# Decoder trunk with hierarchical experts: running sum of x held in four PSUM banks, 21 weight slots, down weights loaded behind the next set's up weights

## The reference, cut to what matters

```
x = x + concat(diff_attention(h), stick_breaking(h)) @ w_out      # h = rms_norm(x) @ w_in
h2 = rms_norm(x)
combine[token, expert] = router weights: best of 4 groups, then best 2 of its 8 experts
x = x + sum over 32 experts e of
        (silu(h2 @ w_gate[e]) * (h2 @ w_up[e]) * combine[:, e]) @ w_down[e]
```

## Time and profile before

| | us |
|---|---|
| median of 3 runs (752.16 to 755.38) | 753.58 |
| the profiled execution | 752.93 |
| its span, first to last instruction | 751.1 |
| PE busy | 662.4 (88%) |
| DVE busy | 302.4 (40%) |
| ACT busy | 126.0 (17%) |
| share of the DMA engines taken by the weight queue | 79.7% |

### The profile page before, as it was taken

How to read it: one execution, slowest core, us unless ns; L and a number is a source line. 1 busy time by engine, 2 the same in 40 slices (tenths; PEclk the granted TensorE clock), 3 DMA queues, 4 the chain that set the end, 5 groups by cost and what they waited for, 6 DMA issues and landing times.

```text
span 751.1 us, 12265 instructions
## 1 busy us (share of the span) xinstructions
PE 662.4 (88%) x4720; PEld 359.2 (48%) x4721; DVE 302.4 (40%) x617; ACT 126.0 (17%) x298; POOL 8.5 (1%) x18
## 2 busy tenths in 40 slices
PE   7999999998898896595899999999887989975856
PEld 4444556475554452432344454656744535523522
DVE  0345654154453542331325267421633435432413
ACT  3114442220000000000031154314100010000000
POOL 0000200000000000000020000000000000000000
PEclk8999999999999998987999999999999999988979
DMA  8796635546999999999999531394289999999995
GB/s 314 247 368 267 160 113 224 219 173 244 419 421 422 421 422 421 422 422 420 361 361 399 229 115 54 136 368 176 82 361 421 423 391 419 422 422 422 421 405 221
DMA packets 52918, 239.05 MB, mean 318 GB/s; under 512 B 7760, under 2 KB 8048, under 8 KB 29328
## 3 DMA queue, kind: packets, MB, share of 16 engines
q1 hardware_dynamic: 52416, 238.09, 79.7%
q0 software_dynamic: 464, 0.47, 0.9%
HBM read 237.49 MB, written 1.05 MB: 318 GB/s over the span
## 4 chain that ended last, share of the span: by engine, by line
PE 67%; DMA 19%; DVE 5%; issue 4%; SPq 2%; DVEq 2%; ACT 1%; ACTq 0%
PE bank L1153 21%; DMA wbuf<-in_w_down 18%; PE bank L1338 11%; PE bank L1306 8%; PE bank L1250 7%; PE bank L1350 5%; PE bank L1281 5%; PE bank L1317 2%; DMA wbuf<-in_w_in 1%; PE bank L1230 1%; PE bank L1173 1%; SPq L355 1%; PE bank L1210 1%; PE bank L1257 1%; PE bank L1184 1%
## 5 line engine op out<-in xcount | busy, mean ns | idle before, releaser
L1153 PE MATMUL bank<-wbuf,hTbuf 128*128 128x512 f32 x384 | 171.2, 602 | 4.1 <-DMA wbuf<-in_w_in 3.7
L1338 PE MATMUL bank<-wbuf,qkT 128*32 128x512 f32 x512 | 73.3, 721 | 54.0 <-DMA wbuf<-in_w_down 47.2
L1153 PEld LDWEIGHTS bank<-wbuf,hTbuf 128*128 128x128 f32 x384 | 72.6, 193 | 91.8 <-issue 87.8
L1306 PE MATMUL bank<-wbuf,qkT 128*32 128x256 f32 x2048 | 113.8, 380 | 2.3 <-DVE qkT L843 2.3
L1306 PEld LDWEIGHTS bank<-wbuf,qkT 128*32 128x32 f32 x2048 | 65.2, 110 | 54.3 <-issue 10.6
L1281 PE MATMUL bank<-qkT,xn 128*128 128x128 f32 x512 | 63.0, 282 | 10.6 <-issue 9.8
L879 DVE TENSOR_TENSOR x_sb<-x_sb,bank 128x512 f32<-128x512 f32 x72 | 49.5, 687 | 50.9 <-PE bank L1350 50.9
L1281 PEld LDWEIGHTS bank<-qkT,xn 128*128 128x128 f32 x512 | 59.9, 196 | 17.8 <-issue 17.8
L1338 PEld LDWEIGHTS bank<-wbuf,qkT 128*32 128x32 f32 x512 | 17.3, 129 | 100.0 <-issue 90.9
L1250 PE MATMUL bank<-wbuf,hTbuf 128*128 128x512 f32 x128 | 56.0, 593 | 0.0
L871 DVE COPY qkT<-bank 128x512 f32<-128x512 f32 x16 | 11.1, 692 | 78.9 <-PE bank L1338 78.9
(11 more groups left out here) (213 smaller groups left out, 577.1 us busy)
## 6 DMA issues: line engine op xcount, KB each, us to landing
wbuf<-in_w_gate SPq DMA_DIRECT2D x64, 1024.0 KB, 14.3
wbuf<-in_w_up SPq DMA_DIRECT2D x64, 1024.0 KB, 18.2
wbuf<-in_w_down SPq DMA_DIRECT2D x56, 1024.0 KB, 14.1
wbuf<-in_w_in SPq DMA_DIRECT2D x24, 1024.0 KB, 14.5
wbuf<-in_w_out SPq DMA_DIRECT2D x8, 1024.0 KB, 7.0
wbuf<-in_w_down SPq DMA_DIRECT2D x16, 512.0 KB, 7.8
x_sb<-in_x SPq DMA_DIRECT2D x2, 512.0 KB, 6.0
out<-x_sb SPq DMA_DIRECT2D x2, 512.0 KB, 2.6
```

The costliest lines, as they stand in the source:

```text
L1153: last = MM(ps[PROJ_BANK[i][t]][:, :], hT[:, k, t * P:(t + 1) * P], block_rows(i, k), start=(k == 0), stop=(k == KC - 1))
L1306: last = MM(ps[bank][j * SLOTS:(j + 1) * SLOTS, 0:FF], hgT[:, k, j * SLOTS:(j + 1) * SLOTS], halves[:, at[j], k, :], start=(k == 0), stop= ...
L1338: last = MM(ps[banks[h]][j * SLOTS:(j + 1) * SLOTS, :], src[:, c, j * SLOTS:(j + 1) * SLOTS], at[j][:, c * D + h * HALF:c * D + (h + 1) * ...
```

## The change

SBUF: `xn` and `hTbuf` move into slots 19 and 20 of `wbuf`. The fourth up piece of odd sets and the first down piece of odd sets get these slots, so they can be loaded earlier. The normed x is written over `x_sb`, and `gather` reads it there with a stride of 8 floats. A further round uses the same `hgT` and `y` as the first round.

PSUM: banks 4 to 7 hold x for a whole layer. `keep_x` writes it there (a matmul with the identity, `start=True`), each scatter accumulates onto it, and after the last set DVE and ACT copy it back to `x_sb`. `into_x`, `x_moe` and `x_more` go. The other work shares banks 0 to 3.

SP: ups of set g+1 are loaded as soon as `up_used` allows, then three downs of set g and the first down of set g+1.

Core of the diff:

```diff
-SLOTS_W = 19
+SLOTS_W = 21
+SLOT_STAGE, SLOT_VALUES, SLOT_SCRATCH, SLOT_XN, SLOT_HT = 13, 14, 15, 19, 20
-UP_SLOT = [[4, 5, SLOT_STAGE, 9], [6, 7, 8, 9]]
-DOWN_SLOT = [10, 11, SLOT_VALUES, 16]
+UP_SLOT = [[4, 5, SLOT_STAGE, 9], [6, 7, 8, SLOT_XN]]
+DOWN_SLOT = [[10, 11, SLOT_VALUES, 16], [SLOT_HT, 11, SLOT_VALUES, 16]]
...
                 load_gate(l, 1, 2)
+                sp_.wait_ge(oT_ps, l * 4 + 4)
+                load_up(l, 1, 3)
                 sp_.wait_ge(oproj_ps, l * 4 + 3)
...
                 load_up(l, 1, 2)
+                sp_.wait_ge(lg_ps, (l + 1) * TT)
+                load_down(l, 1, 0)
...
                 for g in range(1, SETS):
-                    if g > 1:
-                        sp_.wait_ge(up_used, l * SETS + g)
-                        load_up(l, g, LANES - 1)
                     if g + 1 < SETS:
                         sp_.wait_ge(gate_used, l * SETS + g)
                         for j in range(LANES):
                             load_gate(l, g + 1, j)
-                    if g == 1:
                         sp_.wait_ge(up_used, l * SETS + g)
-                        load_up(l, g, LANES - 1)
+                        for j in range(LANES):
+                            load_up(l, g + 1, j)
                     sp_.wait_ge(dn_used, l * SETS + g)
                     if g + 1 < SETS:
-                        for j in range(LANES):
+                        for j in range(1, LANES):
                             load_down(l, g, j)
-                        for j in range(LANES - 1):
-                            load_up(l, g + 1, j)
+                        load_down(l, g + 1, 0)
                     else:
                         for h in range(2):
-                            for j in range(LANES):
+                            for j in range(1, LANES):
                                 load_down_half(l, g, j, h)
...
+            def keep_x(t):
+                for h in range(2):
+                    last = MM(ps[X_BANK[t][h]][:, :], ident, x_sb[:, t, h * HALF:(h + 1) * HALF], start=True, stop=False)
+                last.then_inc(x_kept, 1)
...
-                        last = MM(ps[k // 4][:, (k % 4) * P:(k % 4 + 1) * P], xn[:, t, k * P:(k + 1) * P], sel[:, t, :],
+                        last = MM(ps[k // 4][:, (k % 4) * P:(k % 4 + 1) * P], x_chunked[:, t, k, :], sel[:, t, :],
...
+            def scatter(s, n, weights, h, last):
+                pe.wait_ge(s["y_a" if h else "y_d"], n)
+                for t in range(TT):
+                    mm = MM(ps[X_BANK[t][h]][:, :], weights[:, t, :], y[:, h * HALF:(h + 1) * HALF], start=False, stop=last)
...
+            def downs_and_scatters(s, n, parity, src, weights, second_half, last=False):
+                pe.wait_ge(s["actT_out"], n)
+                pe.wait_ge(s["selwT_out"], n)
+                down(s, n, parity, src, 0)
+                if last:
+                    scatter(s, n, weights, 0, last)
+                down(s, n, parity, src, 1, second_half)
+                if not last:
+                    scatter(s, n, weights, 0, last)
+                scatter(s, n, weights, 1, last)
...
                 def further(m, r):
-                    pe.wait_ge(x_moe, n)
-                    pe.wait_ge(x_more, m)
-                    gather(more, m, sel_more)
-                    pe.wait_ge(first["selwT_out"], n)
-                    transpose_weights(more, m, more_half, selw_more)
+                    gather(more, m, n, sel_more)
+                    pe.wait_ge(first["act_out"], n)
+                    transpose_weights(more, m, SELW_MORE_BANK, selw_more)
                     gate_up_more(m, parity)
...
-                keep_clock(12)
+                for t in range(TT):
+                    keep_x(t)
                 ranks(l)
```

More of the change, by code:

```diff
@@ L241, in decoder @@
         dn_in, last_dn_in = sem("dn_in"), sem("last_dn_in")
+        dn0_in = [sem(f"dn0_in{p}") for p in range(2)]
         out_done = sem("out_done")
@@ L702, in _ @@
                         expert_set(l, pair, parity)
+                act.wait_ge(x_ps[1][1], l + 1)
+                nc.scalar.copy(x_sb[:, 1, HALF:], ps[X_BANK[1][1]][:, :]).then_inc(x_tile[1], 1)
         @block.vector
@@ L927, in expert_set @@
                     act_copy(more, m, ps[MORE_ACT][:, 0:FF], actT_more)
-                    y_copy(more, m, MORE_DN[0], y_more)
-                y_copy(first, n, FIRST_DN[0], y)
-                with dve.If(most > SLOTS):
-                    into_x(more, dve.snap(begun))
-                    gap().then_inc(x_more, 1)
-                for t, add in enumerate(into_x(first, n)):
-                    add.then_inc(x_tile[t], 1)
-                gap().then_inc(x_moe, 1)
-            dve.sem_inc(x_moe, 1)
-            dve.sem_inc(x_more, 1)
+                    y_copy(more, m)
+                y_copy(first, n)
             V.memset(xn[:, 0, 0:P], 0.0).then_inc(zeros_ready, 1)
@@ L1328, in transpose_act @@
                 last.then_inc(s["actT_ps"], 1)
-            def down(s, n, banks, src, second_half=None):
-                pe.wait_ge(s["actT_out"], n)
-                at = [slot(DOWN_SLOT[j]) for j in range(LANES)]
-                for h in range(2):
-                    if h == 1 and second_half is not None:
-                        pe.wait_ge(last_dn_in, second_half)
-                    for c in range(FC):
-                        for j in range(LANES):
-                            last = MM(ps[banks[h]][j * SLOTS:(j + 1) * SLOTS, :], src[:, c, j * SLOTS:(j + 1) * SLOTS],
-                                      at[j][:, c * D + h * HALF:c * D + (h + 1) * HALF], start=(c == 0), stop=(c == FC - 1))
-                            if c == FC - 1:
-                                last.then_inc(s[f"dn{h}_ps"], 1)
@@ L1343, in scatter, with down @@
-            def scatter(s, n, weights, src):
-                pe.wait_ge(s["selwT_out"], n)
-                pe.wait_ge(s["y_d"], n)
-                for t in range(TT):
-                    for h in range(2):
-                        if t == 0 and h == 1:
-                            pe.wait_ge(s["y_a"], n)
-                        MM(ps[SC_BANK[t][h]][:, :], weights[:, t, :], src[:, h * HALF:(h + 1) * HALF],
-                           start=True, stop=True).then_inc(s[f"sc{t}{h}_ps"], 1)
+            def down(s, n, parity, src, h, second_half=None):
+                if h == 1 and second_half is not None:
+                    pe.wait_ge(last_dn_in, second_half)
+                at = [slot(DOWN_SLOT[parity][j]) for j in range(LANES)]
+                for c in range(FC):
+                    for j in range(LANES):
+                        last = MM(ps[DN_BANK[h]][j * SLOTS:(j + 1) * SLOTS, :], src[:, c, j * SLOTS:(j + 1) * SLOTS],
+                                  at[j][:, c * D + h * HALF:c * D + (h + 1) * HALF], start=(c == 0), stop=(c == FC - 1))
+                        if c == FC - 1:
+                            last.then_inc(s[f"dn{h}_ps"], 1)
@@ L1403, in expert_set @@
                     transpose_act(more, m, MORE_ACT, act_more)
[L1404 to L1412 removed]
+                    pe.wait_ge(first["actT_out"], n)
+                    downs_and_scatters(more, m, parity, actT_more, selwT_more, second_half)
+                if parity == 0:
+                    downs_and_scatters(first, n, parity, actT, selwT, None)
+                else:
+                    with pe.If(pair < SETS // 2 - 1):
+                        downs_and_scatters(first, n, parity, actT, selwT, None)
+                    with pe.If(pair >= SETS // 2 - 1):
+                        downs_and_scatters(first, n, parity, actT, selwT, l * 48 + 49, last=True)
             x_chunked = x_sb[:, :, :].rearrange("p t (c k) -> p t k c", k=KC)
```

199 lines of the change are left out of this document (88 added, 111 removed).

## The result

The changed kernel takes **814.67 us** (median of 4 runs, 813.98 to 817.08) against 753.24 for the kernel before: ratio **1.080, 95% interval 1.078 to 1.083**. The direction was forecast. The size was not: +61 us where +13.5 was predicted, and the range ended at 775.

What follows compares the result with a forecast made beforehand. Each layer was taken as bound by DMA's piece stream (2.488 us each) until set 6's downs land, then PE's tail. Layer 0 +6.8 and layer 1 +6.7 give +13.5 on 752.9: 766.4 us, range 757 to 775.

Steps and rivals of the forecast that it cites:

- The stride, priced at 0: In the gather: reading its stationary operand at a stride of 8 floats was taken to cost 0.
- the "other end" of 1.6: Upper bound for the gather's stride: 50 ns on each of 32 loads, 1.6 us per gather.
- The rival: Stride costs 1.6 us per gather, in each layer's first gather and three before set 4's gates: 776 us, chance 0.06.
- The rival on instruction fetch: One fetch stall of PE in each layer's tail, behind the last set's new branch: 775.4 us, chance 0.08.
- The order: Downs behind ups in the load queue: set 6's last down lands 9.95 us later per layer against the stream's end.
- The rival that the order costs nothing: Each layer ends with its stream, not set 6's downs, so 19.9 us would not come: 746.5 us, chance 0.12.
- The early pieces: Fourth up and first down of set 1 load before the router ends: 5.0 us less per layer.
- The hole of 3.3 us in layer 1: DMA stream runs dry before set 4's gates, which wait for set 2's further round: 3.3 us more in layer 1.
- that case (763.1): If the 4.52 us PE stall before set 1's gather in layer 1 vanishes, the new hole closes: 763.1 us.
- The last set's scatters: In the last set each scatter waits for its copy with nothing between: 1.9 us more per layer.
- keep_x: Before `ranks`, at the expert phase's start, its matmuls replace filler: 0.25 us more per layer, bounds 0 and 0.9.
- Dropping `into_x` at nothing: Removing `into_x` and its waits was costed at nothing: DVE is 40% busy and PE waits for DMA anyway.

Runs made afterwards that it cites:

- e2_short: Changed kernel with the stride kept, but the last set's downs written once and shared, 64 PE instructions fewer in the loop body: 783.42 us.
- e3_both: Changed kernel with contiguous gather reads and the last set's downs sharing the other sets' code, 64 instructions fewer: 759.36 us.
- e5: Kernel before, with only the gather reading the normed x at a stride of 8 floats: 776.29 us.
- e7: Kernel before, with 25 never-run float32 matmuls (100 PE instructions) added in the loop: 804.20 us.
- e8: Changed kernel with 37 never-run matmuls (148 instructions) ahead of both layers' loops, so the loops only shift: 835.92 us.
- e12: e3_both with 16 never-run matmuls (64 instructions) added to the loop's body: 779.43 us.
- e9_mixed: e3_both with ups loaded ahead of downs before set 5 and downs ahead of ups from set 5 on: 739.70 us.
- e6: Kernel before, with three ups of the next set loaded ahead of the current set's downs: 769.02 us.
- e11: e3_both with the change's end of the last set, scatter 0 between the halves of the downs: 763.25 us.
- e4: e3_both with each set's three downs loaded ahead of the next set's ups: 750.77 us.

## Why the prediction was wrong, point by point

**The stride, priced at 0, is the first failed step.** The prediction took it from the transposes of `x_sb`, whose strided loads average 191 ns where contiguous ones take 141, and argued that 191 is no more than a gather's 196. It compared two kinds of load. A transpose has one load record, a float32 matmul two (32 for the gather's 16), and each kind has a contiguous price of its own: 141 and 196 ns. Why the same stride adds 50 ns to the one and 140 to the other no run tells. Measured: 335 against 192 ns on a load, 7.8 against 3.8 us on a gather, so +4.0 and not the "other end" of 1.6, which was 50 ns a load. The rival had the right places (the first gather, the gathers before the gates of set 4) and the wrong size, and its chance of 0.06 was too small for a cost whose only evidence was a poor stand-in. With 4.0 its own sum gives 4.0 + 12 - 3 = 13 in layer 0; the stretches up to downs 6 show 11.7 over the forecast. In layer 1 it gives 16, and e2_short, which has the stride alone, shows 9: there the three gathers before the gates of set 4 make these only 6.3 us later than in e3_both, where PE waited 4.62 us for DMA before the downs of set 1. The Trainium skill, "SBUF — State Buffer", section "Door 1: The DMA port swizzle", says that accesses which leave a 16-byte line each pay a penalty. The runs agree with it here (e5), and the prediction should have given that more weight.

**The loop's length was not a step at all, and the second failure.** The rival on instruction fetch named the mechanism, from the 4.52 us gap, but looked for it at a new branch in the tail and charged one stall for each tail. What counts is that the body of a loop grew: seven gaps of 2.5 to 5.6 us in layer 1 (28.1 us), spread over its passes, in the tail only one of them (2.55, with 1.55 behind it). The prediction said nothing of the duplicated block's size, though the order of instructions showed it behind a branch of its own, and it left out what a pause of PE does to the granted clock behind it (0.57, and 10.0 us for a step of 7.11). The Trainium skill, "Runtime: NRT & Kernel Launch", section "Instruction fetch mechanics", says that a taken branch to a page that is not loaded forces a fetch. The packets (22, 50, 77) and the gaps agree as far as they go. The same section says that crossing from one block of instructions to the next is "mostly hidden". The gap inside a gather, with no branch near, shows that this does not hold for these loops. That the boundary is a number of blocks which the loop touches would fit e7, e8 and e12, but no run shows it directly.

**The order held.** Four pieces instead of eight behind the downs of set 6, 71 pieces ahead: forecast 180.9, 181.8 in e3_both. For 67 pieces the same sum gives 171.0, measured 171.6 and 171.0 in e9_mixed. Between the two the four pieces measure 10.2 and 10.9 us, where 9.95 was forecast. The rival that the order costs nothing is refuted by e6 (+14.5). In the changed kernel itself the term is hidden in layer 1, where PE is the bound.

**The early pieces held.** They are in the 75 of that count. The hole of 3.3 us in layer 1 did not come in e3_both: the 4.52 gap shrank to 1.02, the gates of set 4 came 60.6 after the first, and the stretch was 181.9 instead of 184.2. The prediction's remark on that case (763.1) is what e11 measures with 763.25, and not by luck: its six stretches are 174.8, 181.7, 27.4, 163.8, 181.0 and 31.8, where the forecast without the hole has 175.0, 180.9, 28.8, 163.9, 180.9 and 31.8. In the change itself the hole came, and was some 16 us long.

**The last set's scatters held.** Forecast 1.9 per layer, measured 0.86 + 0.87 as waits and 3.9 for both layers (e11).

**keep_x held** as far as rows show it. In the change its eight records take

```profile
158.68 3.68 PE L1246 MATMUL bank<-x_sb,cst 128*128 128x512 f32 x8
```

against 3.79 assumed, and the gates come at 173.5 in e3_both. The 0.25 itself is not shown: kernels that are alike up to there have their first gates up to 2 us apart (173.4 in e12, 175.8 in e4).

**Dropping `into_x` at nothing held** as far as stretches show it: with 45 us less of DVE, e3_both's stretches are what the count of pieces gives.

Put together, the sum without its two missing terms forecasts 766.4, or 763.1 with the gap gone, and the kernel with neither (e11) takes 763.25. The terms that were worked out were right in sign, place and nearly in size; the two left at zero cost 51 us (814.67 against 763.25), and all the others together 13.5 by the forecast.

## What to carry to other kernels

A change that alters how an operand is laid out needs the price of a read at that stride for that operand, loads and moving data apart; where no row shows it, the far end must be wide and its chance not small. Count the instructions that an edit adds to a loop's body, run or not: e3_both shows none of the long gaps in layer 1, and 64 instructions more cost 20 us here, so duplicating a block to vary one flag can be dear. A pause of PE is also paid in the clock of the work behind it. Where a queue is one list, count the pieces behind the transfer that the tail hangs on: keep that number high at the end, and use the other order early, where buffers come free late.

## What the runs showed of the hardware

- A weight load of 128x128 float32 for a gather's matmul takes 335 ns when its source is read with a stride of 8 floats, and 192 to 196 ns contiguous, in either kernel and from either tile.
- Never-run instructions in a loop cost 20 us (64 of them, e12) and 50 us (100, e7), by PE gaps of up to 5.6 us while the instruction queue goes from 22 to 50 and 77 packets. Moving the loops by 148 instructions moved the gaps from layer 1 to layer 0 (e8). The traffic itself is small, 0.82 MB for 50 packets.
- Behind a PE gap of 5 us the granted clock averaged 0.57 over the window from 752 to 760 of the change, and 128 rows of gates and ups took 10.0 us instead of 7.11.
- A gap of 2.57 us before the downs of the further round stands in e3_both, e8 and e12 alike; it has cause issue but does not depend on the length, and its cause was not looked into.
